# Hybrid encoder layer on one core: identity and filter inputs loaded with their neighbours, and the head of the kernel written in another order

## The chip, the cores and the metric

The kernel runs on one core of a Trainium2 chip. The metric is the device time in microseconds of one execution. "Before" is the kernel as it stood, "after" the changed one.

## What is computed

One encoder layer for two request groups (512 tokens and 256 tokens, 768 in all) with one set of weights, width 1024, then a last norm. Cut to what the head of the kernel needs:

```python
mod = c_act @ w_ada[l] + b_ada[l]
sh1, sc1, g1, sh2, sc2, g2 = jnp.split(mod, 6, axis=-1)
h = modulate(rmsnorm(x, norm1_g[l]), sh1, sc1)      # h * (1 + scale) + shift
proj = h @ w_in[l]                                   # attention, Hyena branch, gates
...
z = jnp.concatenate([t, jnp.cos(fr * w), -jnp.sin(fr * w)], axis=-1)   # positions, 33 wide
h = jnp.sin(f1 * (z @ w1 + b1))                      # implicit filter, layer 0
h = jnp.sin(f2 * (h @ w2 + b2))                      # layer 1
h = (h @ w3)
```

The rest (windowed attention, long convolutions through a transform, merge, squared-ReLU MLP, final norm) comes behind it and is not touched.

## The kernel before, in words

Each of the five engines has one instruction list, written out by hand in the order in which it runs; semaphores join them. Activations lie transposed: 128 features by 768 tokens to a slice, `KD` = 8 slices (`k` = 0 to 7). An output tile `t` is the product of one weight tile (512 KB, 8 slices of 128x128) with all slices. Full precision is had by splitting each operand in a high and a low part: for each slice, three products (`w_hi` with the high activations, `w_hi` with the low ones, `w_lo` with the high ones) in two column pieces, six matmuls into `acc_ps` (line 750). Two tiles (slots 0 and 1 of `acc_ps`) are made side by side in the head, by `first(s, k)` for slot `s` and slice `k` (L901 and behind); the third tile has buffers of its own (`w_third_hilo`), and with it begins the plain run of tile after tile.

The head, up to the third tile, has these parts:

- *Loads.* SyncE's queue: the small vectors `vecT`, the even slices of x, then modulation pieces and the first weight tiles. GpSimd's queue: the odd slices of x and the other modulation pieces. ScalarE's queue: the 128x128 identity (`ident`, L1270), the filter's two first weights (L1271), the positions (`filt_zh`, 33 rows, L1272) and the attention sink. The modulation weights for shift and scale of the first norm come in 16 pieces of 512 KB: group `g` (0 to 3) has pieces 4g to 4g+3 and serves slices 2g and 2g+1. Eleven pieces have room at once; the later ones reuse the places of the first.
- *Norm.* ScalarE squares the eight slices of x (`square`, L1298); VectorE sums them (`norm_acc`, `n_acc`, L1751 and L1754); TensorE sums over the features (`norm_sum`, L816); ScalarE takes the root, VectorE the reciprocal (L1770), TensorE spreads it over the partitions (`norm_spread`, L824). VectorE multiplies each slice (`norm_t`, `xT_in`, L1783), ScalarE scales and shifts it (`norm_h`, `n_h`, L1322) and rounds it (`norm_hi`, `act_hilo`, L1328), VectorE makes the low part (`norm_lo`, L1787).
- *Modulation.* For each group TensorE multiplies eight pieces' halves (`mod_row`, L789), ScalarE copies the rows (`mod_rows`, L1361), TensorE turns them (`mod_turn`, L797), VectorE adds biases (`mod_out`, L1817 to L1820). `norm_h` of slices 2g and 2g+1 waits for group g.
- *Filter.* Layer 0: products of positions and weights (`filt_mlp(0)`, L846), then on VectorE the argument of the sine reduced to one turn in seven steps over 768 columns (`arg_first` L1857, `arg_turns` L1865 and L1866, `arg_rest` L1874, `arg_clamp` L1879 and L1880), the sine on ScalarE (L1372). Layer 1 the same (`filt_mlp(1)`, L848).
- *Unread products.* `warm(n)` (L803) multiplies the identity by ones, 256 columns, and nobody reads the result. Ten of them stand between the sums of squares. In the trace each is two records.

ScalarE loads a function table (`ACT_TABLE_LOAD`) where it changes between sigmoid, root and sine; three times in the head.

## Time and profile before

| | us |
|---|---|
| median of 3 timed runs | 1111.06 (1111.06 to 1111.72) |
| the profiled execution's own time | 1114.14 |
| its span in the profile | 1112.6 |
| TensorE busy | 1092.2 |
| VectorE busy | 802.3 |
| ScalarE busy | 454.5 |

The span runs from the first to the last instruction; the execution's own time has about 1.5 us around it. Matmul records are modelled at their ends and overlap, so a busy TensorE is not one at its peak; a line of the timeline merges neighbouring records of one kind.

### The profile page before, as it was taken

To read this page: it belongs to the slowest core of one execution; us is meant where nothing else is said; L and a number is where in the kernel's file an instruction comes from. 1 tells how busy PE (TensorE), PEld (TensorE's weight loads), DVE (VectorE), ACT (ScalarE), POOL (GpSimd) and SP (SyncE) were. 2 spreads that over 40 slices of the span, in tenths; PEclk is the share of its full clock that TensorE was granted. 3 is DMA by queue.
4 is the path that set the end of the run, shared out by engine and by line. 5 is a ranking of instruction groups with operands and counts; after the bars stand their busy time and mean duration, and the time that the engine had idled before them with its cause. 6 is when DMAs were issued, how large, how long until landed. Compare 5 with 4: busy or idle time off the path is not lost.

```text
span 1112.6 us, 16634 instructions
## 1 busy us (share of the span) xinstructions
PE 1092.2 (98%) x6304; PEld 1022.2 (92%) x6304; DVE 802.3 (72%) x1334; ACT 454.5 (41%) x792; POOL 108.9 (10%) x132
## 2 busy tenths in 40 slices
PE   6999999999999999999999999999999999999997
PEld 4787798888899999999899999999999999999886
DVE  5777699889388685556455777787978778788534
ACT  5631156665722322423246232253442526157414
POOL 2101200000334322000000000000000000000000
PEclk9999999999999999999999999999999999999998
DMA  9923454333332333753312331143333232222303
GB/s 345 394 86 117 154 189 143 129 127 114 119 123 105 119 104 124 282 153 108 110 57 95 125 121 57 57 152 99 111 103 106 95 109 91 87 76 76 95 19 115
DMA packets 45525, 138.85 MB, mean 125 GB/s; under 512 B 5051, under 2 KB 10635, under 8 KB 44556
## 3 DMA queue, kind: packets, MB, share of 16 engines
q1 hardware_dynamic: 29024, 80.21, 21.6%
q0 software_dynamic: 11376, 44.84, 11.3%
q10 hardware_dynamic: 5052, 12.81, 3.3%
q8 instruction: 47, 0.77, 0.3%
q14 instruction: 26, 0.21, 0.1%
HBM read 121.61 MB, written 15.74 MB: 123 GB/s over the span
## 4 chain that ended last, share of the span: by engine, by line
PE 93%; DVE 4%; DMA 1%; ACT 1%; issue 0%; ACTq 0%; DVEq 0%
PE acc_ps L750 39%; PE wk L1181 16%; PE acc_ps L1200 12%; PE acc_ps L832 12%; PE wk L1056 2%; PE acc_ps L839 1%; PE wk L991 1%; PE wk L980 1%; PE wk L970 1%; PE wk L1022 1%; PE wk L872 1%; PE wk L885 1%; DVE dot_out L1832 1%; DMA filt_zh<-in_t_z 1%; PE wk L803 1%; PE wk L890 1%
## 5 line engine op out<-in xcount | busy, mean ns | idle before, releaser
L750 PE MATMUL acc_ps<-act_hilo,w_hi 128*128 128x384 f32 x1504 | 332.5, 342 | 0.1
L750 PEld LDWEIGHTS acc_ps<-act_hilo,w_hi 128*128 128x128 f32 x1504 | 264.8, 189 | 18.8 <-issue 17.7
L750 PE MATMUL acc_ps<-act_hilo,w_lo 128*128 128x384 f32 x752 | 191.5, 335 | 0.0
L750 PEld LDWEIGHTS acc_ps<-act_hilo,w_lo 128*128 128x128 f32 x752 | 136.4, 188 | 0.0
L1200 PE MATMUL acc_ps<-hidden_hilo,act_hilo 128*128 128x384 f32 x768 | 134.6, 335 | 0.2
L1200 PEld LDWEIGHTS acc_ps<-hidden_hilo,act_hilo 128*128 128x128 f32 x768 | 133.2, 188 | 1.1 <-issue 1.1
L1741 DVE TENSOR_TENSOR w_lo<-w_raw,w_hi 128x1024 fp32r<-128x1024 f32 x61 | 76.3, 1252 | 55.1 <-ACT w_hi L1282 54.1
L1282 ACT ACTIVATE w_hi<-w_raw 128x1024 fp32r<-128x1024 f32 x61 | 64.2, 1053 | 44.3 <-PE acc_ps L750 40.9
L2198 DVE SCALAR_TENSOR_TENSOR xT<-acc_ps,modT,xT 128x512 f32<-128x512 f32 (+1 forms) x32 | 19.7, 617 | 59.7 <-PE acc_ps L832 59.5
L1832 DVE CUSTOM_DVE_ANT_0 dot_out<-dot_ring,c_rows,vecT 128x1024 f32<-128x1024 f32 x48 | 61.6, 1284 | 1.6 <-issue 0.6
L2323 DVE SCALAR_TENSOR_TENSOR xT<-acc_ps,modT,xT 128x384 f32<-128x384 f32 (+2 forms) x96 | 40.5, 478 | 28.8 <-PE acc_ps L1200 28.8
L750 PE MATMUL acc_ps<-hidden_hilo,w_hi 128*128 128x384 f32 x256 | 54.7, 334 | 0.0
L1515 ACT ACTIVATE gates_out<-acc_ps 128x768 f32<-128x768 f32 x16 | 13.0, 813 | 98.3 <-PE acc_ps L750 98.3
L832 PE MATMUL acc_ps<-hidden_hilo,w_down_hilo 128*128 128x512 f32 (+1 forms) x288 | 50.2, 336 | 0.0
L832 PEld LDWEIGHTS acc_ps<-hidden_hilo,w_down_hilo 128*128 128x128 f32 x288 | 44.4, 190 | 5.6
L1181 PE MATMUL wk<-act_hilo,w_hi 128*128 128x384 f32 x192 | 48.7, 334 | 0.0
L1181 PE MATMUL wk<-t_hilo,w_hi 128*128 128x384 f32 x192 | 48.7, 334 | 0.0
L2305 DVE TENSOR_TENSOR c_st<-wk,c_st 128x384 f32<-128x384 f32 x84 | 44.9, 551 | 2.7 <-PE wk L1181 2.3
L750 PEld LDWEIGHTS acc_ps<-hidden_hilo,w_hi 128*128 128x128 f32 x256 | 45.3, 188 | 0.0
L1614 ACT ACTIVATE act_hilo<-w_raw 128x512 fp32r<-128x512 f32 x32 | 20.0, 626 | 59.0 <-PE acc_ps L1200 59.0
L2312 DVE TENSOR_TENSOR hidden_hilo<-c_st,hidden_hilo 128x384 fp32r<-128x384 f32 x48 | 26.8, 558 | 22.5 <-ACT hidden_hilo L1633 22.2
L1605 ACT ACTIVATE w_hi<-s_sum 128x512 fp32r<-128x512 f32 x24 | 14.9, 628 | 64.1 <-DVE s_sum L2280 64.1
(301 smaller groups left out, 2026.4 us busy)
## 6 DMA issues: line engine op xcount, KB each, us to landing
w_raw<-in_w_pre SPq DMA_DIRECT2D x50, 512.0 KB, 3.5
dot_ring<-in_w_ada_cols POOLq DMA_DIRECT2D x48, 512.0 KB, 3.8
w_raw<-in_w_up SPq DMA_DIRECT2D x32, 512.0 KB, 3.7
w_raw<-in_w_down SPq DMA_DIRECT2D x16, 512.0 KB, 3.4
w_raw<-in_w_down_half SPq DMA_DIRECT2D x32, 256.0 KB, 2.7
spec<-filt_out POOLq DMA_DIRECT2D x12, 512.0 KB, 2.9
gate_spill<-gates_out ACTq DMA_DIRECT2D x16, 384.0 KB, 2.3
hy_spec<-spec SPq DMA_DIRECT2D x12, 512.0 KB, 5.6
```

Source lines behind the costliest of these rows:

```text
L750: mm = pe.matmul(acc_ps[:, slot, 512 * h:512 * h + HALF], w[:, k, :], src[:, x, k, HALF * h:HALF * h + HALF], start=(first and i == 0), st ...
L832: mm = pe.matmul(acc_ps[:, slot, half(h)], w_i[:, k, :], src[:, x, k, half(h)], start=(n == 0 and i == 0), stop=(n == KD - 1 and i == 2))
L1056: mm = pe.matmul(wk[:, c + o:c + o + P], w, x, start=(i == 0), stop=(i == 1))
L1181: mm = pe.matmul(st_ps(q, j), w[:, k, :], st_act(j, x, k), start=(k == 0 and i == 0), stop=(k == PK - 1 and i == 2))
L1200: mm = pe.matmul(acc_ps[:, m % 2, 512 * h:512 * h + HALF], w[:, k, :], hid[:, x, k, HALF * h:HALF * h + HALF], start=(k == 0 and i == 0), ...
L1282: act_e.activation(whi[s][:] if to is None else to[0], raw[s][:], ACT.Copy).then_inc(hi_done, 1)
L1614: act_e.activation(st_weight(ST_DOWN[m % 3])[0], quarter(m % 4), ACT.Copy).then_inc(sd_hi, 1)
L1741: dve.tensor_tensor(lo, raw[s][:], hi, ALU.subtract).then_inc(lo_done, 1)
L1832: dve.tensor_tensor_reduce(junk[:], ring[:, i], cb[:, g], 1.0, vT[:, V_BA + mt:V_BA + mt + 1], ALU.mult, ALU.add, modT[:, mt, g:g + 1]).th ...
L2305: dve.tensor_tensor(dst, st_ps(q, j), other, ALU.add).then_inc(st_u, 1)
L2312: dve.tensor_tensor(hid_block(q, b, 1), c_block(b), hid_block(q, b, 0), ALU.subtract).then_inc(h4_lo, 1)
L2323: last = dve.scalar_tensor_tensor(xT[:, m, a:b], acc_piece(s, a, b), modT[:, G2 + m, g:g + 1], xT[:, m, a:b], ALU.mult, ALU.add)
```

## The change

1. The identity becomes 128 further columns of the vectors' file (`vecT`), and is no load of its own. The positions and the filter's two weights become one file of 64 rows of 960 numbers (`filt_in`), one load, first in ScalarE's queue. The positions are computed as before, in a function `positions`.
2. SyncE's list: modulation piece 3 moves to it from GpSimd's list, the first weight tile stands behind pieces 1 and 3, the second behind 5 and 7.
3. TensorE: layer 0's products first; layer 1's between the sums of squares in place of unread products (six of the ten stay ahead of the norm); two rows of group 0 ahead of the norm's sum; four unread products, into `acc_ps`, between the halves of group 1's rows; the second weight tile's first products each one place earlier.
4. VectorE: layer 0's argument steps among the first two sums of squares, layer 1's first three steps around the reciprocal.
5. ScalarE: the sine's table first, then the root's behind the squares, then the sine's again behind `act_hilo` of slice 5; layer 0's sine between the squares; rows of group 0 copied ahead of the first weight tile's split, the second tile's split behind the rows of group 1.

```diff
@@ sync
             sp.dma_start(vT[:], a["vec"]).then_inc(ld_vec, 16)
             for k in range(0, KD, 2):
                 x_load(sp, k)
-            mod_load(sp, 1)
+            for p in (1, 3):
+                mod_load(sp, p)
             weights(0)
+            for p in (5, 7):
+                mod_load(sp, p)
             weights(1)
-            for p in range(5, 4 * MODS, 2):
+            for p in range(9, 4 * MODS, 2):
                 mod_load(sp, p)
@@ gpsimd
-            for p in (0, 2, 3, *range(4, 4 * MODS, 2)):
+            for p in range(0, 4 * MODS, 2):
                 mod_load(pool, p)
@@ tensor
-            pe.wait_ge(ld_ident, 16)
+            pe.wait_ge(ld_filt, 16)
+            filt_mlp(0)
+            pe.wait_ge(ld_vec, 16)
             turn_c()
-            pe.wait_ge(ld_filt, 32)
-            filt_mlp(0)
             pe.wait_ge(ones_set, 2)
-            for k in range(2, KD - 1):
+            for k in range(2, 6):
                 pe.wait_ge(n_acc, k)
-                warm(2)
+                if k == 3:
+                    pe.wait_ge(f_sin, 1)
+                    filt_mlp(1)
+                else:
+                    warm(2)
+            for k in range(2):
+                mod_row(0, k)
             norm_sum(0)
-            for k in range(KD):
+            for k in range(2, KD):
                 mod_row(0, k)
             norm_spread(0)
             mod_turn(0)
             for k in range(4):
                 mod_row(1, k)
-            pe.wait_ge(f_sin, 1)
-            filt_mlp(1)
+            warm(4, acc_ps[:, 0, 0:256])
             for k in range(4, KD):
                 mod_row(1, k)
             first(0, 0)
             mod_turn(1)
             first(0, 1)
+            first(1, 0)
             for k in range(KD):
                 mod_row(2, k)
-            first(1, 0)
+            first(1, 1)
             mod_turn(2)
             first(0, 2)
-            first(1, 1)
@@ scalar
-            act_e.dma_start(ident[:], a["t_ident"]).then_inc(ld_ident, 16)
-            act_e.dma_start(fw12[:], a["filt_w12"]).then_inc(ld_filt, 16)
-            act_e.dma_start(zh[0:33, :], a["t_z"]).then_inc(ld_filt, 16)
+            act_e.dma_start(fin[:], a["filt_in"]).then_inc(ld_filt, 16)
...
-            act_e.activation(rs[:, 0:1], epsc[:], ACT.Sqrt).then_inc(sqrt_set, 1)
+            act_e.activation(es[:, 0, 0:1], epsc[:], ACT.Sin)
+            square(0)
+            square(1)
             act_e.wait_ge(c_turned, 1)
...
-            for k in range(KD):
+            square(2)
+            square(3)
+            act_e.wait_ge(f_arg, 1)
+            act_e.activation(h1[:], fb[0:64, :], ACT.Sin).then_inc(f_sin, 1)
+            for k in range(4, KD):
                 square(k)
+            act_e.activation(rs[:, 0:1], epsc[:], ACT.Sqrt).then_inc(sqrt_set, 1)
             act_e.wait_ge(sqrt_set, 1)
             norm_std(0)
-            act_e.activation(es[:, 0, 0:1], epsc[:], ACT.Sin)
+            mod_rows(0)
             split_w(0)
-            mod_rows(0)
-            split_w(1)
-            act_e.wait_ge(f_arg, 1)
-            act_e.activation(h1[:], fb[0:64, :], ACT.Sin).then_inc(f_sin, 1)
             norm_h(0)
             norm_hi(0)
             norm_h(1)
             norm_hi(1)
             mod_rows(1)
+            split_w(1)
...
             norm_hi(5)
+            act_e.activation(es[:, 0, 0:1], epsc[:], ACT.Sin)
@@ vector
-            for k in range(KD):
-                norm_acc(k)
             arg_first(0)
             arg_turns(0)
+            norm_acc(0)
+            arg_rest(0)
+            norm_acc(1)
+            arg_clamp(0)
+            for k in range(2, KD):
+                norm_acc(k)
+            arg_first(1)
             norm_rstd(0)
-            arg_rest(0)
-            arg_clamp(0)
+            arg_turns(1)
             norm_t(0)
...
             mod_out(1)
-            arg_first(1)
             split_w(1)
...
             norm_t(5)
-            arg_turns(1)
             norm_lo(4)
```

On TensorE, the head of its list up to the spread of the norm. Before (line, operation, out<-in, shape and count; `ident` is the identity, `mod_raw` and `c_padded` make the rows of the modulation):

```order
L809 MATMUL wk<-ident,c_act 16x128
L846 MATMUL acc_ps<-filt_zh,filt_w 64x512
L846 MATMUL acc_ps<-filt_zh,filt_w 64x256
L803 MATMUL wk<-ones,ident 128x256 x10
L816 MATMUL wk<-ones,n_acc 128x1 x6
L789 MATMUL wk<-mod_raw,c_padded 32x512 x8
L824 MATMUL wk<-ident,norm_rstd 128x128 x6
```

and after:

```order
L849 MATMUL acc_ps<-filt_in 64x512
L849 MATMUL acc_ps<-filt_in 64x256
L812 MATMUL wk<-vecT,c_act 16x128
L806 MATMUL wk<-ones,vecT 128x256 x2
L851 MATMUL acc_ps<-filt_h,filt_in 128x512
L851 MATMUL acc_ps<-filt_h,filt_in 128x256
L806 MATMUL wk<-ones,vecT 128x256 x4
L792 MATMUL wk<-mod_raw,c_padded 32x512 x2
L819 MATMUL wk<-ones,n_acc 128x1 x6
L792 MATMUL wk<-mod_raw,c_padded 32x512 x6
L827 MATMUL wk<-vecT,norm_rstd 128x128 x6
```

Layer 1's products and two rows of group 0 now stand ahead of the norm's sum, four of the unread products no longer do.

On VectorE, the same place, from the first sum of squares to the first normalised slice. Before:

```order
L1751 COPY n_acc<-n_sq 128x768
L1754 TENSOR_TENSOR n_acc<-n_acc,n_sq 128x768 x7
L1857 TENSOR_SCALAR filt_arg<-acc_ps,vecT 64x768
L1865 TENSOR_SCALAR filt_turn<-filt_arg 64x768
L1866 TENSOR_SCALAR filt_turn<-filt_turn 64x768
L1770 RECIPROCAL norm_rstd<-norm_rstd 128x6
L1874 SCALAR_TENSOR_TENSOR filt_red<-filt_turn,filt_arg 64x768
L1874 SCALAR_TENSOR_TENSOR filt_red<-filt_turn,filt_red 64x768
L1879 SCALAR_TENSOR_TENSOR filt_red<-filt_turn,filt_red 64x768
L1880 TENSOR_SCALAR filt_red<-filt_red 64x768
L1783 TENSOR_TENSOR xT_in<-xT_in,wk 128x768
```

and after, to the reciprocal:

```order
L1868 TENSOR_SCALAR filt_arg<-acc_ps,vecT 64x768
L1876 TENSOR_SCALAR filt_turn<-filt_arg 64x768
L1877 TENSOR_SCALAR filt_turn<-filt_turn 64x768
L1762 COPY n_acc<-n_sq 128x768
L1885 SCALAR_TENSOR_TENSOR filt_red<-filt_turn,filt_arg 64x768
L1885 SCALAR_TENSOR_TENSOR filt_red<-filt_turn,filt_red 64x768
L1765 TENSOR_TENSOR n_acc<-n_acc,n_sq 128x768
L1890 SCALAR_TENSOR_TENSOR filt_red<-filt_turn,filt_red 64x768
L1891 TENSOR_SCALAR filt_red<-filt_red 64x768
L1765 TENSOR_TENSOR n_acc<-n_acc,n_sq 128x768 x6
L1868 TENSOR_SCALAR filt_arg<-acc_ps,vecT 128x768
L1781 RECIPROCAL norm_rstd<-norm_rstd 128x6
```

All seven steps of layer 0 now stand ahead of the last six sums, and the first step of layer 1 ahead of the reciprocal.

On ScalarE, the last slices of the norm. After:

```order
L1328 ACTIVATE n_h<-xT_in,modT,norm_scale 128x512
L1328 ACTIVATE n_h<-xT_in,modT,norm_scale 128x256
L1363 ACTIVATE mod_rows<-wk 128x512
L1334 ACTIVATE act_hilo<-n_h 128x768
L1398 ACT_TABLE_LOAD
L1398 ACTIVATE att_sinke<-eps 128x1
L1328 ACTIVATE n_h<-xT_in,modT,norm_scale 128x512
L1328 ACTIVATE n_h<-xT_in,modT,norm_scale 128x256
```

The first two rows are slice 5, the last two slice 6; the table load and the one-column sine between them are new here, the rest stood so before.

## Rows read from the trace of the kernel before

**Rows 1.** The page: the span, and TensorE's busy time

```profile
span 1112.6 us, 16634 instructions
...
PE 1092.2 (98%) x6304; PEld 1022.2 (92%) x6304; DVE 802.3 (72%) x1334; ACT 454.5 (41%) x792; POOL 108.9 (10%) x132
```

**Rows 2.** Busy time by stretches (us): PE, PEld, DVE, ACT, POOL, clock, DMA share, GB/s

```profile
20.00:25.00 5.00, 5.00 (x43) 3.44 (x43) 4.39 (x8) 4.00 (x6) 1.05 (x2) 1.00 1.03 409
...
56.00:1106.00 1050.00, 1046.48 (x6062) 988.91 (x6060) 760.00 (x1266) 415.47 (x736) 96.30 (x103) 1.00 0.33 111
```

**Rows 3.** The chain that ended last, 0 to 70 us: start, us, what

```profile
1.91 7.76 DMA filt_zh<-in_t_z
...
9.71 2.82 PE acc_ps L846 x4
12.53 7.12 PE wk L803 x20
...
46.08 21.13 PE acc_ps L750 x120
```

**Rows 4.** Line 803, the unread products: duration ns min/median/max, first and last start

```profile
L803 PE MATMUL wk<-ones,ident x20: 379/634/795, 12.5 to 19.3; 128*128 128x256 f32 x20
```

**Rows 5.** Busy time by stretches, columns as in rows 2, around the clock's fall

```profile
34.90:38.20 3.30, 2.17 (x18) 1.81 (x14) 2.44 (x4) 2.52 (x4) 0.00 (x0) 1.00 1.02 402
38.30:41.60 3.30, 3.30 (x12) 3.30 (x12) 3.00 (x7) 2.16 (x4) 2.58 (x5) 0.50 0.79 265
```

**Rows 6.** Timeline of VectorE: start us, us, what, idle before and its releaser

```profile
16.70 2.02 DVE L1754 TENSOR_TENSOR n_acc<-n_acc,n_sq 128x768 f32<-128x768 f32 x2 [0.30 <-ACT n_sq L1298]
...
18.64 1.06 DVE L1857 TENSOR_SCALAR filt_arg<-acc_ps,vecT 64x768 f32<-64x768 f32 x1
...
21.35 0.19 DVE L1770 RECIPROCAL norm_rstd<-norm_rstd 128x6 f32<-128x6 f32 x1 [0.48 <-ACT norm_rstd L1313]
...
24.84 0.94 DVE L1783 TENSOR_TENSOR xT_in<-xT_in,wk 128x768 f32<-128x768 f32 x1
```

**Rows 7.** Timeline of ScalarE, columns as in rows 6

```profile
15.82 1.58 ACT L1298 ACTIVATE n_sq<-xT_in 128x768 f32<-128x768 f32 x2 [0.74 <-DMA xT_in<-in_x_T]
...
21.26 1.28 ACT L1367 ACT_TABLE_LOAD   x1
22.55 0.20 ACT L1367 ACTIVATE att_sinke<-eps 128x1 f32<-128x1 f32 x1
...
27.48 0.84 ACT L1328 ACTIVATE act_hilo<-n_h 128x768 fp32r<-128x768 f32 x1
...
47.20 1.31 ACT L1322 ACTIVATE n_h<-xT_in,modT,norm_scale 128x512 f32<-128x512 f32 x2 [1.68 <-issue]
```

**Rows 8.** Timeline of TensorE, columns as in rows 6

```profile
19.48 1.40 PE L816 MATMUL wk<-ones,n_acc 128*128 128x1 f32 x12
...
28.55 1.14 PE L789 MATMUL wk<-mod_raw_b,c_padded 128*32 128x512 f32 x8
...
30.94 1.05 PE L797 MATMUL wk<-vecT,mod_rows 128*128 128x2 f32 x8
...
37.38 1.11 PE L797 MATMUL wk<-vecT,mod_rows 128*128 128x2 f32 x8 [1.14 <-ACT mod_rows L1361]
...
42.12 1.48 PE L789 MATMUL wk<-mod_raw,c_padded 128*32 128x512 f32 x10
...
45.13 0.95 PE L797 MATMUL wk<-vecT,mod_rows 128*128 128x2 f32 x8
...
56.53 8.59 PE L750 MATMUL acc_ps<-act_hilo,w_third_hilo 128*128 128x384 f32 x48
```

**Rows 9.** DMA issues up to 60 us (KB, us to landing), and GpSimd's wait

```profile
ident<-in_t_ident ACTq DMA_DIRECT2D x1, 64.0 KB, 2.4
...
sink<-in_attn_sink ACTq DMA_DIRECT2D x1, 4.0 KB, 10.1
...
38.27 0.53 POOL L621 DMA_DIRECT2D filt_w<-in_filt_w  x1 [14.60 <-DMA mod_raw_c<-in_w_ada_rows]
```

More of the change, by code:

```diff
@@ L2529, in _, with positions @@
                     y_half(k - 1)
+def positions():
+    import numpy as np
+    f = np.float32
+    zs = []
+    for L in (TS, TP):
+        t = np.linspace(0.0, 1.0, L, dtype=f)
+        w = (f(2.0 * PI) * np.arange(L, dtype=f) / f(L)).astype(f)
+        fr = np.linspace(1e-4, 15, 16, dtype=f)
+        fw = (fr[:, None] * w[None, :]).astype(f).astype(np.float64)
+        zs.append(np.concatenate([t[None].astype(np.float64), np.cos(fw), -np.sin(fw)], axis=0))
+    return np.concatenate(zs, axis=1).astype(f)
 def tables():
```

53 lines of the change are left out of this document (24 added, 29 removed).

## The prediction, made before the changed kernel ran

> **What bounds the kernel now.** I read the page first: TensorE is busy 1092.2 of 1112.6 us [rows 1]. The busy time by stretches says where the rest lies: from 56 to 1106 us it is busy 1046.5 of 1050 us [rows 2]. So whatever the change does, it does in the head, and it is worth as much as it moves one event: the first product of the third weight tile, at 56.53 us [rows 8]. From there on TensorE works through an unchanged list.
>
> The chain of waits through the head begins with a transfer: the positions of the filter land 7.76 us after their issue at 1.91 us, then four products take 2.8 us, then twenty records of the unread products 7.1 us [rows 3]. These last are at half speed to begin with: one takes 634 ns in the middle case and 379 ns in the fastest [rows 4]. The profile's clock column prints 1.00 there, but the durations show 1.2 GHz until about 17.7 us, after TensorE had worked since 9.7 us; then it is at 2.4 GHz. It falls once more: 0.50 from 38.3 to 41.6 us, after the stretch 34.9 to 38.2 in which TensorE was busy only 2.17 of 3.3 us [rows 5]; it sat idle 1.14 us for the copied rows of modulation group 2 [rows 8]. The fall costs about half of 3.4 us, 1.7 us.
>
> From 46.1 us on the chain is TensorE alone [rows 3]. Before that, it goes through VectorE and ScalarE: sum of squares ready at 18.7 us, first normalised slice begun at 24.84 us [rows 6], and each slice then through `n_h` and `act_hilo` on ScalarE [rows 7]. The last modulation piece has landed by 38.3 us, when GpSimd stops waiting for it [rows 9]; group 3's rows start only at 42.12 us [rows 8], so the transfers do not bound the end of the head.
>
> **The change, part by part.**
>
> *Loads.* Three transfers of 211 KB on ScalarE's queue become one of 64 rows of 3,840 bytes (240 KB), the vectors grow from 81 to 145 KB: 93 KB more, 0.23 us at the 409 GB/s of 20 to 25 us [rows 2]. When the filter's file lands, no row shows. Lower bound: like the unit matrix, also first in that queue, 2.4 us after its issue at 0.9 us [rows 9], so 3.3 us. Upper: like the positions, 7.8 us after issue, so 8.7 us. It is first in its queue and has only 4 rows for each of 16 engines, so it is nearer the first: I take 3.9 us.
>
> *Filter, layer 0.* Four products of 2.8 us end at 6.7 us. VectorE's seven argument steps took from 18.64 to 24.84 us less the reciprocal of 0.19 us and the 0.48 us of waiting ahead of it, 5.5 us [rows 6], behind the sums of squares. Now they stand ahead of sums 3 to 8. 6.7 + 5.5 + two sums (0.6 and 1.0) and the waits between them end at 13.9; six sums every 1.06 us (two take 2.02 [rows 6]) end at 20.2 us. Before it was 18.7 us: the transfer of x, whose last pair of squares starts at 15.82 [rows 7], no longer bounds this, VectorE does: **+1.5 us**.
>
> *TensorE before the norm.* Six unread products instead of ten stand ahead of the sum, but layer 1's products now too, and two rows of group 0. Sine ready at about 14.7; layer 1 has as many records and columns as layer 0, which took 2.8 us with its tail at 1.2 GHz [rows 3], so 2.6 us to the next product, to 17.3; four unread products are eight records, 3.4 us at 1.2 GHz or 1.7 us at full clock (634 - 379 is the 0.2 us by which one is longer [rows 4]). If the clock rises at about 19.5 us, they end at 20.2, two rows take 0.9: the sum starts at 21.1 us instead of 19.48 [rows 8], **+1.6 us**. (A rise at 17.7 gives 20.3, none before 21.2 gives 22.2.)
>
> *From the norm to group 3.* The spread moves by the same 1.6. But VectorE had held the first `xT_in` until 24.84 [rows 6] with arguments that are now done, so that one moves only to 25.8 (+1.0), and the turn of group 1 goes from 30.94 [rows 8] to 32.0 (+1.1). Landings: a piece of 512 KB takes 1.28 us at 409 GB/s, 2.56 us while two queues share. The last of x landed at 15.8 [rows 7], 16.05 now; SyncE's list behind it (pieces 1, 3, weight 0, 5, 7, weight 1, 9) gives weight 1 at 31.4, needed at 33, and piece 9 at 34.0; then GpSimd's queue is done, and 11 follows at 35.5, 15 at 38.1. Rows of group 2 run 35.7 to 37.5, behind slice 0 of the second tile, which followed them before. Then the second tile's slice 1 (1.04 us) fills the 1.14 us of idleness, and the clock need not fall: group 3's rows start at 40.5, not 42.12, **-1.6 us**.
>
> *The unread four* (1.7 us, from 27.5 us) end at 29.2 while TensorE would wait for the last piece of group 1, which before came at about 28.6 [rows 8] and now 0.24 later, and for VectorE. They cost nothing; without that cover they would cost at most 1.7.
>
> *What is late next.* Rows of group 3 end at 42.3, but ScalarE copies them only behind `n_h` of slice 5. That one follows the scale of group 2 (ready on VectorE at 40.2) by two `n_h` (1.3 us each) and one `act_hilo` (0.8) [rows 7]: copy 43.6 to 44.2. So the turn moves from 45.13 only to 44.3: **-0.8 us**. From there 10.4 us of products in either kernel lead to the third tile: its start 56.53 becomes 55.7 us. VectorE finishes the last slices one ahead of TensorE, by about 0.7 us as now.
>
> *Table loads.* Four instead of three, 1.28 us each and 0.2 for what follows [rows 7]. The sine's stands ahead of the first square, as the root's did; the root's lies after the last square, while TensorE works; the new one, 1.5 us, lies behind `act_hilo` 5, where ScalarE was idle for 1.68 us [rows 7]: nothing. In the rows the next operation starts 1.29 us after the load began. The Trainium skill (ScalarE: Activation LUTs, What ACT_TABLE_LOAD costs) adds a drain of some 1.4 us to each switch; the trace does not bear it out. By it slices 6 and 7 would be 1.2 us later with 0.7 us of slack, so the sum 0.5 us worse.
>
> **The sum.** -0.8 us against the profiled execution's own 1114.14 us. The timed runs lie 3.1 us below that one, at 1111.06 us. Whether they had the fall of 1.7 us is not recorded. If they had, the forecast is 1110.3; if not, their third tile began at 54.8 and the change makes it 55.7: 1112.0. In the middle **1111.2 us**. No change, that is: about 0.2% (2.2 us) is what a measurement tells from none.
>
> **Rivals.**
>
> *Slower: the clock rises late.* Now TensorE worked without a break from 9.71 until 17.7 us before it rose. After the change it has layer 0's products until 6.7, nothing until about 12.3, two unread products, a gap, and layer 1's with 64 of 128 rows. If it stays at 1.2 GHz until 24.6 us, the sum starts at 22.2, its 12 records take 2.3 instead of 1.4 us, the six rows 3.4 instead of 1.7, and the third tile starts at about 58.1: +1.6 against the profiled execution, up to +3.3 against runs without the fall, 1114.2 us. It decides from a rise later than about 23 us. For it: the durations of [rows 4]. Against: from 14.7 us TensorE has no gap. The Trainium skill (TensorE: Matmul & The Clock Gate, HAM oscillation) says that gaps between bursts send the clock back to half; the fall at 38.3 us agrees. Chance 0.15.
>
> *Late file.* It lands like the positions did, at 7 us or later. Everything of VectorE's moves with it: sums of squares at 23.1, third tile at 57.7 to 58.2, in time 1112.5 to 1114.0, so 1113.3. For it: even the 4 KB of the sink took 10.1 us [rows 9]; against: those were last in the queue. Chance 0.10.
>
> *Faster.* File at 3.5, clock full by 17.7, third tile at 54.8, and the copy of group 3 not behind `n_h` 5, another 1.1 us: -2.8 us against runs that have the fall, 1108.3 us. For it: 1.7 us of cold clock and 1.14 us of waiting are there to be had [rows 5, 8]. Against: the copy's place in ScalarE's order. Chance 0.12 (0.13 with a little less).
>
> *It does not keep the clock up.* The unread four lie at 27 to 29 us, the fall at 38 us; only the second tile's moved product fills that place. Should the clock fall anyway, 1.7 us come back: 1112.9 us. This lies inside the forecast's 0.62.
>
> **Chances.** Forecast 0.62, all within 0.2%. Late clock 0.15: 0.12 slower, 0.03 same. Late file 0.10: 0.06 and 0.04. Faster 0.13: 0.12 and 0.01. So faster 0.12, same 0.70, slower 0.18. The range takes in the late clock and the edge of the faster case: 1108.9 to 1114.5 us.
>
> **What would show it.** The filter's file landed by 4 us (layer 0's products start there); last sum of squares at about 20; TensorE's sum of them at 21; records of the unread products at 634 or 379 ns; no 0.50 in the clock column at 38 us; group 3's rows at 40.5; the third tile at 55.7. A third tile before 54.3 or after 57.9, or a different idle time behind 56 us, would make the prediction wrong.

## The result, and the profile after

The changed kernel takes **1117.88 us** (median of 6, 1117.33 to 1120.74); the kernel before took 1111.39 us beside it (1111.01 to 1113.94). The ratio is 1.0056, 95% interval 1.0041 to 1.0071: some 6 us slower, where no change was forecast. The profiled execution took 1117.58 us. Its page, span and busy time, as in [rows 1]:

```profile
span 1115.9 us, 16636 instructions
...
PE 1092.6 (98%) x6304; PEld 1020.1 (91%) x6304; DVE 802.0 (72%) x1334; ACT 456.4 (41%) x794; POOL 108.4 (10%) x131
```

The engines do the same work. The busy time by stretches of the changed kernel, columns as in [rows 2]:

```profile
9.00:14.00 5.00, 0.00 (x0) 0.00 (x0) 4.83 (x8) 1.60 (x3) 0.00 (x0) 1.00 1.03 411
...
59.00:1109.00 1050.00, 1046.02 (x6058) 988.51 (x6058) 759.31 (x1265) 415.00 (x735) 96.30 (x103) 1.00 0.34 111
...
38.30:41.60 3.30, 3.30 (x25) 1.61 (x24) 1.82 (x2) 2.24 (x5) 2.16 (x5) 1.00 0.98 330
```

Behind 59 us TensorE is as busy as before, and there is no fall of the clock at 38 us. TensorE does nothing at all from 9 to 14 us, while VectorE is busy for 4.83 of these 5 us. What it does shows on its timeline (columns as in rows 6):

```profile
8.38 1.07 DVE L1868 TENSOR_SCALAR filt_arg<-acc_ps,vecT 64x768 f32<-64x768 f32 x1 [3.72 <-PE acc_ps L849]
...
10.66 0.56 DVE L1762 COPY n_acc<-n_sq 128x768 f32<-128x768 f32 x1
...
13.10 0.96 DVE L1765 TENSOR_TENSOR n_acc<-n_acc,n_sq 128x768 f32<-128x768 f32 x1
...
14.95 0.55 DVE L1891 TENSOR_SCALAR filt_red<-filt_red 64x768 f32<-64x768 f32 x1
15.43 6.26 DVE L1765 TENSOR_TENSOR n_acc<-n_acc,n_sq 128x768 f32<-128x768 f32 x6
...
25.66 0.19 DVE L1781 RECIPROCAL norm_rstd<-norm_rstd 128x6 f32<-128x6 f32 x1 [2.99 <-ACT norm_rstd L1319]
...
28.68 0.95 DVE L1794 TENSOR_TENSOR xT_in<-xT_in,wk 128x768 f32<-128x768 f32 x1 [1.80 <-PE wk L827]
```

The last six sums run back to back and end at 21.7 us: VectorE is the engine that is late, no longer the transfer of x. Behind them it has spare time, 2.99 and 1.80 us, where before it made the first `xT_in` late. ScalarE waits for it with the squares, which have two buffers:

```profile
11.32 0.84 ACT L1304 ACTIVATE n_sq<-xT_in 128x768 f32<-128x768 f32 x1 [1.56 <-DVE n_acc L1762]
14.15 0.84 ACT L1304 ACTIVATE n_sq<-xT_in 128x768 f32<-128x768 f32 x1 [1.99 <-DVE n_acc L1765]
15.54 0.84 ACT L1374 ACTIVATE filt_h<-filt_red 64x768 f32<-64x768 f32 x1 [0.54 <-DVE filt_red L1891]
...
48.06 1.28 ACT L1398 ACT_TABLE_LOAD   x1
49.35 0.20 ACT L1398 ACTIVATE att_sinke<-eps 128x1 f32<-128x1 f32 x1
49.73 1.31 ACT L1328 ACTIVATE n_h<-xT_in,modT,norm_scale 128x512 f32<-128x512 f32 x2 [0.17 <-issue]
```

And TensorE's timeline, the places of [rows 8]:

```profile
5.53 2.82 PE L849 MATMUL acc_ps<-filt_in 33*64 33x512 f32 x4 [5.53 <-DMA filt_in<-in_filt_in]
...
14.20 2.05 PE L806 MATMUL wk<-ones,vecT 128*128 128x256 f32 x4 [5.32 <-DVE n_acc L1765]
16.52 2.90 PE L851 MATMUL acc_ps<-filt_h,filt_in 64*128 64x512 f32 x4 [0.27 <-ACT filt_h L1374]
19.35 3.43 PE L806 MATMUL wk<-ones,vecT 128*128 128x256 f32 x8
22.71 1.05 PE L792 MATMUL wk<-mod_raw,c_padded 128*32 128x512 f32 x4
23.70 1.50 PE L819 MATMUL wk<-ones,n_acc 128*128 128x1 f32 x12
...
30.28 1.99 PE L806 MATMUL acc_ps<-ones,vecT 128*128 128x256 f32 x8
...
37.49 0.93 PE L753 MATMUL acc_ps<-act_hilo,w_hi 128*128 128x384 f32 x4 [0.48 <-issue]
...
47.36 1.05 PE L800 MATMUL wk<-vecT,mod_rows 128*128 128x2 f32 x8 [0.46 <-ACT mod_rows L1363]
...
59.04 2.18 PE L753 MATMUL acc_ps<-act_hilo,w_third_hilo 128*128 128x384 f32 x11
```

From 16.52 to 23.70 us it has no gap, but runs at 1.2 GHz almost to the end: the eight records from 19.35 us take 3.43 us. The trace's record of the clock has its first stretch at full speed from 22.3 us on; the clock column of the views prints 1.00 ahead of that too, as in the kernel before. The norm's sum starts 2.0 us behind the end of the last sum of squares, and 1.0 us of this are the two rows of group 0 (22.71 to 23.70). The filter's file is first in its queue, and in the DMA issues (KB, us to landing) stands

```profile
filt_in<-in_filt_in ACTq DMA_DIRECT2D x1, 240.0 KB, 4.6
```

so it landed at 5.49 us.

### The profile page after: what moved, and what is told of

It is laid out like the page before. It is cut to its first block, busy times and chain, and to the rows that moved or that the text cites. A ratio compares the mean times of both kernels' runs of the same rounds, so it can differ in the third digit from the quotient of the medians.

```text
span 1115.9 us, 16636 instructions
## 1 busy us (share of the span) xinstructions
PE 1092.6 (98%) x6304; PEld 1020.1 (91%) x6304; DVE 802.0 (72%) x1334; ACT 456.4 (41%) x794; POOL 108.4 (10%) x131
## 3 DMA queue, kind: packets, MB, share of 16 engines
q1 hardware_dynamic: 29168, 80.80, 22.3%
## 4 chain that ended last, share of the span: by engine, by line
PE 91%; DVE 3%; ACT 1%; issue 1%; DMA 1%; DVEq 0%; ACTq 0%
PE acc_ps L753 39%; PE wk L1189 16%; PE acc_ps L1208 12%; PE acc_ps L835 12%; PE wk L1064 2%; PE acc_ps L842 1%; PE wk L999 1%; PE wk L988 1%; PE wk L978 1%; PE wk L1030 1%; PE wk L875 1%; PE wk L888 1%; DVE dot_out L1843 1%; PE wk L893 1%; DMA spec<-filt_out 1%
## 5 line engine op out<-in xcount | busy, mean ns | idle before, releaser
L2336 DVE SCALAR_TENSOR_TENSOR xT<-acc_ps,modT,xT 128x384 f32<-128x384 f32 (+2 forms) x96 | 40.5, 478 | 28.8 <-PE acc_ps L1208 28.8
```

What stands on the lines that cost most here:

```text
L2336: last = dve.scalar_tensor_tensor(xT[:, m, a:b], acc_piece(s, a, b), modT[:, G2 + m, g:g + 1], xT[:, m, a:b], ALU.mult, ALU.add)
```

## The experiments

Fourteen runs, e1 to e14. Each time stands against the median of the kernel before on the same chip. The table gives, for the profiled execution of each, where an event starts (us, from the timelines): the last sum of squares on VectorE, the norm's sum and spread and the turns of groups 1 to 3 on TensorE, the third tile. The last column is the start of the first stretch at full speed in the trace's record of the clock.

| kernel | last sum of squares | norm's sum | spread | turn 1 | turn 2 | turn 3 | third tile | clock first rises |
|---|---|---|---|---|---|---|---|---|
| before (1114.14, rows above) | 17.8 | 19.48 | 22.66 | 30.94 | 37.38 | 45.13 | 56.53 | 17.8 |
| e1, before again (1111.64) | 16.8 | 18.51 | 21.69 | 29.97 | 36.41 | 42.59 | 54.05 | 16.0 |
| e6, files only | 17.2 | 18.19 | 21.97 | 30.18 | 36.52 | 42.72 | 54.02 | 16.1 |
| e13, arguments alone | 20.9 | 21.89 | 25.18 | 33.20 | 39.63 | 45.82 | 57.11 | 19.1 |
| after | 20.7 | 23.70 | 26.96 | 34.79 | 41.70 | 47.36 | 59.04 | 22.3 |
| e7, queues back | 20.4 | 24.23 | 27.50 | 35.32 | 42.24 | 47.89 | 59.58 | 23.8 |
| e3, six products more | 20.3 | 21.35 | 25.89 | 34.09 | 42.58 | 48.23 | 59.91 | 13.0 |
| e8, three steps less | 17.7 | 21.83 | 25.10 | 32.93 | 39.84 | 45.49 | 57.17 | 21.0 |
| e9, both of these | 17.5 | 18.56 | 21.83 | 31.03 | 38.12 | 43.77 | 55.46 | 11.5 |
| e10, sum first | 20.0 | 20.98 | 26.78 | 34.60 | 41.53 | 47.18 | 58.88 | 26.3 |
| e5, filter back | 17.4 | 19.22 | 22.49 | 30.78 | 38.79 | 44.45 | 55.85 | 16.1 |
| e11, second tile back too | 17.9 | 19.25 | 22.52 | 30.91 | 37.25 | 43.42 | 54.72 | 15.8 |
| e12, group 2 ahead | 17.2 | 18.19 | 22.54 | 30.32 | 36.10 | 42.18 | 53.47 | 16.1 |
| e14, copies ahead | 17.6 | 18.58 | 22.81 | 30.59 | 35.73 | 41.81 | 53.68 | 16.9 |

### What the profiled execution of before stands for: e1

The kernel before, unchanged, once more.

> The kernel before, unchanged, to see how much of the gap between the two kernels the profiled execution of before hides. In its first trace the clock fell to half from 38.3 to 41.6 us and the third weight tile began at 56.53 us, and that execution took 1114.14 us where the others took 1111.0 to 1111.7. If the fall belongs to the slower executions, as I think, a trace of this kernel without a fall has the third tile at about 54 to 55 us and a time of 1111.1. If the rival holds (the fall is in all of them and the 3 us are the profiler's), the fall shows again, with 1111.1 beside it.

1112.01 against 1112.93 us, ratio 0.9998 (0.9988 to 1.0007). Its profiled execution took 1111.64 us, 2.5 us less than that of [rows 1], and its busy time by stretches around the place of [rows 5] is

```profile
34.10:37.40 3.30, 2.17 (x15) 1.85 (x15) 2.44 (x4) 2.52 (x4) 0.00 (x0) 1.00 1.03 405
37.40:40.70 3.30, 3.30 (x25) 2.35 (x28) 2.85 (x7) 2.23 (x4) 2.68 (x5) 1.00 0.69 217
```

while its timeline of TensorE has

```profile
18.51 1.40 PE L816 MATMUL wk<-ones,n_acc 128*128 128x1 f32 x12
...
36.41 1.05 PE L797 MATMUL wk<-vecT,mod_rows 128*128 128x2 f32 x8 [1.13 <-ACT mod_rows L1361]
...
54.05 2.15 PE L750 MATMUL acc_ps<-act_hilo,w_third_hilo 128*128 128x384 f32 x11
```

The same idle time of 1.13 us and the same 2.17 us of work in 3.3 us, and no fall of the clock. So the fall belongs to a part of the executions of before. This trace, like that of the changed kernel, has no fall in the head, and is the one to compare with: the third tile is 5.0 us later after the change, and 5.2 us of delay are already there at the norm's sum.

### Parts of the change on the kernel before: e2, e6, e13

**e2**: files and queue order of the change, every engine's order as before.

```diff
-            mod_load(sp, 1)
+            for p in (1, 3):
+                mod_load(sp, p)
             weights(0)
+            for p in (5, 7):
+                mod_load(sp, p)
             weights(1)
...
-            for p in (0, 2, 3, *range(4, 4 * MODS, 2)):
+            for p in range(0, 4 * MODS, 2):
```

> The kernel before with the loads of the change alone: the identity in the vectors' file, one file for the filter (lying in another free place), the new order of pieces on the two queues; all engines' lists as before. If the reordered head costs the 6.5 us, this is 1110.5 to 1112 us, with the filter's file at about 5.5 us and the sum of squares at about 19 us. If the loads cost it (piece 9, piece 11 and the second weight land later, x later), it is 1114 or more, with idle time ahead of group 2's rows.

1121.7 against 1112.93 us, ratio 1.008 (1.0065 to 1.0095). ScalarE's timeline:

```profile
31.21 1.06 ACT L1283 ACTIVATE w_hi<-w_raw 128x1024 fp32r<-128x1024 f32 x1 [6.13 <-DMA w_raw<-in_w_pre]
```

The second weight tile now lands behind four pieces, and before's order has its split ahead of slice 0's scaling: 6.13 us of waiting, the clock falls from 26.2 to 39.9 us, third tile at 63.71. That price belongs to the mixture, not to the change, which moves that split.

**e6**: the files only.

```diff
-            act_e.dma_start(ident[:], a["t_ident"]).then_inc(ld_ident, 16)
-            act_e.dma_start(fw12[:], a["filt_w12"]).then_inc(ld_filt, 16)
-            act_e.dma_start(zh[0:33, :], a["t_z"]).then_inc(ld_filt, 16)
+            act_e.dma_start(fin[:], a["filt_in"]).then_inc(ld_filt, 16)
```

> The kernel before with the merged files alone (identity in the vectors' file, one filter file first in ScalarE's queue), queues of pieces and all engines' lists as before. If the 9 to 10 us of the second run were the blocked split of the second weight, this is 1110.5 to 1112.5 us, and the first n_h starts near 25.5 us. If larger files cost by themselves (x or the vectors landing 1 us late), 1113 or more.

1113.03 against 1112.96 us, ratio 0.9999 (0.999 to 1.0009), third tile at 54.02. The merged files are worth nothing by themselves; the file landed at 5.92 us, and from here on e6 serves as the base.

**e13**: e6, and on VectorE alone layer 0's arguments ahead.

```diff
-            for k in range(KD):
-                norm_acc(k)
             arg_first(0)
             arg_turns(0)
-            norm_rstd(0)
+            norm_acc(0)
             arg_rest(0)
+            norm_acc(1)
             arg_clamp(0)
+            for k in range(2, KD):
+                norm_acc(k)
+            norm_rstd(0)
```

> One part of the change alone, on the version with merged files (run e6, which is as fast as before): only VectorE's order, layer 0's seven argument steps ahead of and among the first two sums of squares. Every other engine stays as before (TensorE: the two loads' products, ten unread products, sum; layer 1's products behind the norm; ScalarE: squares, root, split, sine). Theory (VectorE's 5.5 us of arguments push the sums of squares, and the norm's sum with them, and nothing behind gives it back): last sum starts at 20.5 to 21.5 us instead of 17.2, the norm's sum at 22 to 22.5 instead of 18.2 if the clock has risen, third tile 2 to 4 us later (the first normalised slice no longer waits 1 us for arguments, so 3), at 56.5 to 58, time 1115 to 1116.5 against some 1112.5. Rival (the modulation pieces and the split's order bound the head, the norm has slack): third tile at 54 to 55, time as e6.

1115.26 against 1111.85 us, ratio 1.0027 (1.0016 to 1.0037). Timelines of VectorE and TensorE:

```profile
15.58 6.26 DVE L1752 TENSOR_TENSOR n_acc<-n_acc,n_sq 128x768 f32<-128x768 f32 x6
...
14.35 2.04 PE L803 MATMUL wk<-ones,vecT 128*128 128x256 f32 x4 [5.85 <-DVE n_acc L1752]
16.57 4.97 PE L803 MATMUL wk<-ones,vecT 128*128 128x256 f32 x16 [0.18 <-DVE n_acc L1752]
21.89 1.50 PE L816 MATMUL wk<-ones,n_acc 128*128 128x1 f32 x12 [0.35 <-DVE n_acc L1752]
```

VectorE's order alone moves the last sum of squares by 3.7 us and the third tile by 3.1 (57.11 against 54.02); by the ratio, too, it is 3 us slower. The norm has no slack. Its TensorE was idle for 5.85 us too, yet with ten unread products and nothing else ahead of the sum it follows the last sum of squares at once.

### Parts taken off the changed kernel: e3, e8, e9, e10, e7

**e3**: six unread products into the gap.

```diff
             pe.wait_ge(ones_set, 2)
+            warm(6)
```

> The changed kernel with six more unread products right behind layer 0's, where TensorE is idle from 8.9 to 14.2 us. If the late rise of the clock (22.3 us instead of 17.8) costs a good part, the clock rises by 18 to 19 us, the norm's sum starts at 22.6 or earlier instead of 23.7, and 1.5 to 2.5 us come back: 1115.5 to 1116.5. If VectorE's order costs nearly all, the sum of squares still ends at 21.7 us and under 1 us comes back: 1117 or more.

1116.04 against 1112.93 us, ratio 1.003 (1.002 to 1.0041); 11 runs, from 1114.63 to 1119.40. The clock is up at 13.0 us and the norm's sum starts at 21.35, right behind VectorE: 2.35 us earlier than after (0.4 of this because its filter file landed earlier). But the profiled execution, the longest of them, lost the clock twice; by stretches:

```profile
19.50:22.90 3.40, 2.62 (x21) 1.68 (x24) 2.68 (x3) 2.09 (x3) 0.00 (x0) 1.00 1.03 410
23.30:26.70 3.40, 3.40 (x16) 1.08 (x9) 1.19 (x3) 0.68 (x2) 0.94 (x2) 0.50 1.02 407
```

**e8**: three of layer 0's seven steps left out (the filter's values differ).

```diff
             def arg_rest(layer):
+                if layer == 0:
+                    return
...
-                chain(dve.scalar_tensor_tensor(fb[h], fk[h], -TWO_PI_C, fb[h], ALU.mult, ALU.add))
+                if layer:
+                    chain(dve.scalar_tensor_tensor(fb[h], fk[h], -TWO_PI_C, fb[h], ALU.mult, ALU.add))
```

> The changed kernel without three of layer 0's seven argument steps (the two that take off whole turns and the first half of the last; the filter's values are then others). If VectorE's list bounds the sums of squares, they end about 2.9 us earlier, at 18.8 us. If that alone carries on, the third tile starts near 56 us: 1114.5 to 1115.5. If TensorE at half speed is the second bound behind it (six unread products, layer 1 and two rows ahead of the norm's sum), the sum starts only 1.5 to 2 us earlier, and it is 1115.5 to 1116.5.

1115.74 against 1112.96 us, ratio 1.0026 (1.0016 to 1.0035). TensorE:

```profile
17.04 3.78 PE L806 MATMUL wk<-ones,vecT 128*128 128x256 f32 x8
...
21.83 1.50 PE L819 MATMUL wk<-ones,n_acc 128*128 128x1 f32 x12
```

The sums are 3.0 us earlier, the norm's sum and the third tile only 1.9: TensorE, at half speed, ends later than VectorE. So there are two bounds close to each other.

**e9**: e3's and e8's edits together (the same three steps left out).

```diff
             pe.wait_ge(ones_set, 2)
+            warm(6)
...
+                if layer == 0:
+                    return
```

> The kernel after, with both of the edits that each gave back a part: three of layer 0's seven argument steps left out on VectorE (the two of L1885 and the first of L1890; the filter's values differ, so this leaves out part of the computation), and six unread products behind the turn of c, so that TensorE is not idle ahead of the sums. Theory (two bounds on the norm's sum, VectorE's 5.5 us of arguments and TensorE at half speed behind its idleness): the sums end at 18.8 us and TensorE, at full clock, starts the norm's sum within 0.7 us of that, at 19.5; third tile at about 55, time 1113 to 1113.8 against 1115.74 and 1116.04 with one edit each. Rival (one bound only, the other edit's gain is the same gain): 1115.5 to 1116. If the clock falls again in the gap behind the six products: 1115.

1114.63 against 1112.09 us, ratio 1.0024 (1.0014 to 1.0033). The norm's sum starts at 18.56 us, as before, 5.1 us earlier than after: each bound had hidden the other. The third tile gains only 3.6 of it, and the time lay 0.8 us above what I expected. TensorE and ScalarE:

```profile
25.86 1.05 PE L792 MATMUL wk<-mod_raw_b,c_padded 128*32 128x512 f32 x4 [0.66 <-DMA mod_raw_b<-in_w_ada_rows]
...
31.41 1.06 ACT L1289 ACTIVATE w_hi<-w_raw 128x1024 fp32r<-128x1024 f32 x1 [0.81 <-DMA w_raw<-in_w_pre]
```

With the norm as early as before, group 1's piece and the second weight tile land late: the transfers are a third bound. I read this from the two waits; no run takes it away. The rival's size (1115.5 or more) did not come either. By the ratios alone (1.0024 and 1.0026) e9 cannot be told from e8; the norm's sum tells them apart.

**e10**: nothing but layer 1's products between the sine and the norm's sum.

```diff
-            for k in range(2, 6):
+            for k in range(2, 4):
...
-            for k in range(2):
-                mod_row(0, k)
             norm_sum(0)
-            for k in range(2, KD):
+            for k in range(KD):
                 mod_row(0, k)
```

> The kernel after without the unread products behind the fourth and fifth sum and with all rows of group 0 behind the norm's sum, as before: nothing but layer 1's products is between the sine and the norm's sum. Theory (VectorE's late sums are the first bound, at 21.7 us; TensorE's queue adds 1.3 to 2 us): the norm's sum starts at 21.9, but at half speed, since TensorE was idle before it: its twelve records take 2.3 instead of 1.4 us and the rows 3.4 instead of 1.8; third tile 58 to 59, time 1116.5 to 1117.9. Rival (the unread products and the rows are what costs, the rest of the order is harmless): third tile at 57.2, time 1116 or less.

1119.25 against 1112.09 us, ratio 1.0061 (1.0046 to 1.0077).

```profile
17.61 1.06 PE L851 MATMUL acc_ps<-filt_h,filt_in 64*128 64x256 f32 x2
20.98 2.72 PE L819 MATMUL wk<-ones,n_acc 128*128 128x1 f32 x12 [2.32 <-DVE n_acc L1763]
23.63 3.22 PE L792 MATMUL wk<-mod_raw,c_padded 128*32 128x512 f32 x16
26.78 1.60 PE L827 MATMUL wk<-vecT,norm_rstd 128*128 128x128 f32 x12
```

The norm's sum is 2.7 us earlier (0.8 of it because the filter's file landed earlier), the spread behind it only 0.2: sum and rows at 1.2 GHz take 2.72 and 3.22 us, where e13 took 1.50 and 1.92 for them. The clock rises at 26.3 us. From the end of the last sum of squares to the spread it takes 5.9 us, after took 5.3. So the unread products and the two rows cost 2 us in the queue, and leaving them out costs at least as much in the clock. The third tile (58.88) is where the theory had it; the time lies 1.4 us above its range, and by the ratios (1.0061 and 1.0056) e10 cannot be told from after.

**e7**: both queues in the order of before.

```diff
-            for p in (1, 3):
-                mod_load(sp, p)
+            mod_load(sp, 1)
             weights(0)
```

> The changed kernel with the pieces and weights in their old order on SyncE's and GpSimd's queues. If the queue order of the change is harmless to its own lists, as its trace says (rows of group 2 wait for nothing at 38.7 us, long after piece 11 at 33.7), it stays at 1117 to 1118.5 us. If landings bound the changed head, 1116 or less, or above 1119.

1117.49 against 1112.96 us, ratio 1.0042 (1.0027 to 1.0056), third tile at 59.58: the order of the queues is not the cause. This run shows something else as well. Its filter file landed 0.8 us earlier than after's, at 4.7 us, and still its clock rose later, at 23.8 us. TensorE:

```profile
13.87 2.04 PE L803 MATMUL wk<-ones,vecT 128*128 128x256 f32 x4 [5.77 <-DVE n_acc L1762]
19.02 3.78 PE L803 MATMUL wk<-ones,vecT 128*128 128x256 f32 x8
```

The stretch without work is as long as after's (5.77 against 5.32 us), for the arguments and the sums behind it start with the file too.

### The filter back at its place, the other moves kept: e4, e5, e11

**e4**: TensorE, ScalarE and VectorE have the filter's steps where they stood; the two rows ahead of the norm's sum, the second tile's moves and the queues stay.

```diff
-                if k == 3:
-                    pe.wait_ge(f_sin, 1)
-                    filt_mlp(1)
-                else:
-                    warm(2)
+                warm(2)
...
-            warm(4, acc_ps[:, 0, 0:256])
+            pe.wait_ge(f_sin, 1)
+            filt_mlp(1)
```

> The changed kernel with the filter's steps where they were (layer 0's argument behind the sums of squares, its sine behind the split of the weights, layer 1 in group 1's rows, ten unread products, no unread four; ScalarE's and VectorE's lists as before). Loads, layer 0's products first, two rows ahead of the norm's sum and the second tile's products one place earlier stay. If the filter's place on VectorE ahead of the sums is the cause, the sums end at 18.7 to 19 us and it is 1109.5 to 1111.5. If TensorE's moved rows and products are the cause it stays above 1114.

1124.86 against 1112.93 us, ratio 1.0099 (1.0081 to 1.0118), third tile at 66.30. It took ScalarE's list of before whole, and with it e2's blocked split: a mistake of the experiment, so it says nothing on the filter's place. **e5** mends it:

```diff
-            split_w(0)
             mod_rows(0)
-            split_w(1)
+            split_w(0)
...
             mod_rows(1)
+            split_w(1)
```

> The fourth run again (filter's steps back in their old places on VectorE, ScalarE and TensorE, all other moves of the change kept), with one repair: in the fourth run ScalarE's old list asked for the second weight at 25 us, which the new queue order lands at 30 to 31 us; here its split stands behind the rows of group 1, as in the change. If the filter's place ahead of the sums is the cause of the 5 us in the head, the sums end by 18.5 us, the first normalised slice starts at 24 to 25 us, the third tile at 54 to 55.5 us, and it is 1111 to 1113 us. If TensorE's moves or the queue order cost by themselves, the third tile stays at 57 us or later and the time at 1115 or more.

1114.49 against 1112.96 us, ratio 1.0024 (1.001 to 1.0039). The norm's sum is back at 19.22 us and the third tile 3.2 us earlier than after: most of the 5.0 us, but third tile and time lie above both ranges of the theory (55.85 and 1114.49 us). The norm's sum starts 0.8 us behind the end of the last sum of squares (18.39 us), where e6's followed at once: the two rows of group 0, now ahead of it, take 1.0 us. The rest of what remains shows on TensorE:

```profile
34.58 0.93 PE L753 MATMUL acc_ps<-act_hilo,w_hi 128*128 128x384 f32 x4 [1.59 <-DVE w_lo L1744]
...
35.79 1.48 PE L792 MATMUL wk<-mod_raw_b,c_padded 128*32 128x512 f32 x10
```

The second tile's slice 0, now ahead of group 2's rows, waits for the low part of its weights, and the rows wait behind it. **e11** puts it back:

```diff
             first(0, 1)
-            first(1, 0)
             for k in range(KD):
                 mod_row(2, k)
-            first(1, 1)
+            first(1, 0)
             mod_turn(2)
             first(0, 2)
+            first(1, 1)
```

> The kernel with the filter's steps at their old places (run e5, 1114.49 us), and now also the second tile's first two slices at their old places on TensorE: slice 0 behind group 2's rows, slice 1 behind slice 2 of the first tile. Theory (of e5's remaining 1.5 us, most is the second tile's slice 0 ahead of group 2's rows: it waits for the split of the second weight tile, which now stands behind group 1's rows, and the rows stand behind it, 35.8 instead of 32.1 us): group 2's rows at 32 to 33, third tile 54.3 to 54.8, time 1113.0 to 1113.5. Rival (it is the landing of the modulation pieces in the new queue order): group 2's rows stay at 34 or later, time 1114.2 to 1114.8.

1113.22 against 1112.09 us, ratio 1.0009 (0.9999 to 1.0018); group 2's rows start at 32.97 us, third tile at 54.72, 1.1 us earlier than e5. It confirms the place. In the changed kernel itself the same wait is only 0.48 us (at 37.49). There layer 1's argument step is already done, and the weights had the time of the late norm to land; that these are the reasons is argued, not shown.

### A version that beats both? e12, e14

In e1 ScalarE copies the rows of group 2, ready at 34.1 us, only behind slice 3's scaling at 35.78, and TensorE waits 1.13 us for them. **e12** is e6 with this (and slice 3's multiplication ahead of the second tile's split on VectorE):

```diff
-            norm_h(3)
             mod_rows(2)
+            norm_h(3)
...
-            norm_lo(3)
             mod_out(2)
+            norm_lo(3)
```

> A version meant to beat both: the kernel before with the two merged files only (run e6, 1113.03 against 1113.0), and group 2 served sooner. ScalarE copies group 2's rows ahead of slice 3's scaling instead of behind it; VectorE multiplies slice 3 ahead of layer 1's first argument step and the second tile's split, and adds group 2's biases ahead of slice 3's low part. In the trace of the kernel before, undisturbed, the rows of group 2 ended at 34.1, the copy began at 35.8 behind slice 3's scaling, and the turn at 36.4; the biases followed at 38.0 and slice 4 at 38.4. Theory (the head between the spread and the third tile is a chain turn, biases, scaling, not transfers): turn of group 2 at 35, slice 4's scaling at 36.9, third tile 0.8 to 1.5 us earlier, at 52.6 to 53.3, ratio to before 0.9987 to 0.9993. Rival (the pieces of group 3 land at 37 to 38 us and bound the end): turn of group 2 earlier, third tile the same, ratio 1.000.

1111.39 against 1112.09 us, ratio 0.9995 (0.9986 to 1.0004), third tile at 53.47: less than hoped. The turn of group 2 is only 0.4 us earlier than e6's. TensorE now waits 0.60 us for the split instead:

```profile
34.98 0.93 PE L750 MATMUL acc_ps<-act_hilo,w_hi 128*128 128x384 f32 x4 [0.60 <-issue]
```

**e14** leaves slice 3 where it was and serves group 3 in the same way.

```diff
-            norm_h(5)
             mod_rows(3)
+            norm_h(5)
...
-            norm_lo(5)
             mod_out(3)
+            norm_lo(5)
```

> Second try at a version that beats both. Run e12 (1111.39 against 1112.09, ratio 0.9995 with an interval that holds 1) got the turn of group 2 only 0.4 us earlier, since slice 3's multiplication, put ahead of the second tile's split on VectorE, let TensorE wait 0.6 us for that split with slice 0 of the second tile, which stands ahead of the turn. Now VectorE keeps slice 3 where it was; ScalarE copies the rows of group 2 ahead of slice 3's scaling and those of group 3 ahead of slice 5's, and VectorE adds the biases of groups 2 and 3 ahead of slice 3's and slice 5's low part. Theory (the chain turn, biases, scaling bounds the end of the head): turn of group 2 at 35.0, slice 4's scaling at 37, turn of group 3 at 41, third tile at 52.5 to 53.2, 0.8 to 1.5 us ahead of e6's 54.02, ratio 0.9985 to 0.9993. Rival (TensorE waits for the low part of slice 3 instead, since the biases stand ahead of it, or the last piece lands at 37 to 38 us and group 3's rows wait for it): third tile at 53.5 to 54, ratio 0.9995 to 1.

1111.35 against 1111.85 us (11 runs), ratio **0.9992** (0.9983 to 1.0001). ScalarE and TensorE:

```profile
34.80 0.60 ACT L1359 ACTIVATE mod_rows<-wk 128x512 f32<-128x512 f32 x1 [0.49 <-PE wk L789]
35.29 1.30 ACT L1320 ACTIVATE n_h<-xT_in,modT,norm_scale 128x512 f32<-128x512 f32 x2
...
35.73 0.95 PE L797 MATMUL wk<-vecT,mod_rows 128*128 128x2 f32 x8
```

From the spread to the third tile it takes 30.9 us, e6 took 32.0; 0.8 of this was lost ahead of the spread in the profiled execution, half at the norm's sum and half in group 0's rows, which took 2.87 us against 2.42. e12 took 30.9 us as well, so serving group 3 sooner gained nothing more, and the third tile (53.68) lies where the rival had it. It beats the changed kernel by 6 us. That it beats the one before is not shown: the interval just holds 1.

## Why the prediction was wrong

The place was right: everything happens ahead of the third tile, and the chain goes through the norm's sum. The steps:

1. *"I take 3.9 us" for the landing of the filter's file.* It was 5.49 us, 4.6 us after its issue; in the runs with the same file 3.7 to 5.0 us. I had bounds of 2.4 and 7.8 us from [rows 3, 9] and went to the nearer one by its place in the queue, not by its size, which is nearly four times that of the unit matrix. The Trainium skill (DMA: Bandwidth & Descriptors, Anatomy of one DMA) has a fit for transfers that GpSimd issues: some 2.0 us, and the bytes at 436 GB/s. An estimate by it for 240 KB is 2.6 us; this transfer, issued by ScalarE, took 3.7 to 5.0 us while the other queues loaded x.
2. *The sums "end at 20.2 us", "+1.5 us".* They ended at 21.7. The duration of the seven steps (5.5 us) and the six sums behind each other were right; the 1.5 us between are step 1. But the delay was reckoned from 18.7 us, in an execution whose x landed late; in e1 the sums end at 17.8 us, and the delay is 3.9 us, not 1.5. Measured alone (e13), the order of VectorE costs 3.7 us at the last sum and **3.1 us at the third tile**.
3. *"If the clock rises at about 19.5 us … the sum starts at 21.1".* It rose at 22.3 us and the sum started at 23.7. The sine was ready at 16.4 instead of 14.7 us (step 1 again), and from there on layer 1's products (2.9 us), eight records (3.4) and two rows stood in the queue, nearly all at 1.2 GHz. The text gives the sum at 22.2 us for no rise before; with the sine 1.7 us later that is 23.9, and so it came: the size of the case was right, the choice wrong. Beside e13, where VectorE's sums end at nearly the same time (21.8 us, here 21.7), the changed kernel loses another **1.9 us** at the third tile (59.04 against 57.11). This is a difference of two kernels that differ in the queues, in ScalarE's list and behind the norm too; but 1.8 of it is there at the norm's sum, which in e13 follows the last sum of squares at once, and e3 and e9, with TensorE kept busy, have nearly none of it there. So I put it to TensorE's new order. These two are the 5.0 us.
4. *The rivals.* Late clock (0.15) and late file (0.10) were priced one by one, at 1114.2 and 1113.3 us. Neither came as it was set: the file landed 1.6 us late, not 3, and the clock rose at 22.3 us, where the rival wanted a rise behind 23. Half of each came, and the halves add up: what delays the file delays the sine, and with it the queue of TensorE that runs at 1.2 GHz. The late clock is not the file's doing, though: e7's landed 0.8 us earlier and its clock rose 1.5 us later. The two prices were too low as well. Their third tiles, 58.1 and 57.7 to 58.2, mean 1115.7 and 1115.3 to 1115.8 us by step 6. By the text's own reckoning, too, 3.3 us above 1111.06 are 1114.4 us, not 1114.2.
5. *"Group 3's rows start at 40.5, not 42.12", "-1.6 us".* The 42.12 came from an execution with the fall; without it they start at 39.59 (e1). From the norm's sum to the third tile I had 34.6 us; after the change it is 35.3, in e1 35.5. So all that the change does behind the norm's sum gave 0.2 us. The second tile's moves fill the 1.13 us of waiting for the copy of group 2's rows, and group 3's rows start 20.0 us behind the norm's sum instead of e1's 21.1 (forecast 19.4). But at the turn of group 3 0.4 us of this is left (23.7 against 24.1): its rows' copy stands behind slice 5's scaling, as the text had it, and TensorE waits 0.46 us for it.
6. *"If not, their third tile began at 54.8", and the middle of two cases.* e1 took 1111.64 us with the third tile at 54.05, 1057.6 us from there; the profiled execution of [rows 8] has the same 1057.6 us. So a third tile at 55.7 meant 1113.3 us, not 1111.2. This is the step that counted on a gain: 1.5 of the 2.4 us that the text takes off between the norm's sum and the third tile (37.05 to 34.6) are the fall, which by their mean clock more than half of the executions of before did not have. The fall itself is 1.5 of the 2.5 us between the two, about the 1.7 in the text; 1.0 us was there already at the norm's sum (19.48 against 18.51), since x landed later.
7. *The unread four and the table load*, both costed at nothing: the four end at 32.2 us and group 1's rows behind them at 33.2, when slice 0's low part is ready too, without which TensorE's next product (33.32) can't start. The sine's table is followed 1.29 us later by the next operation (48.06, 49.35), without a drain, while TensorE works through slices 4 and 5. No run took them out of the changed kernel by themselves, so for both this is argued from the trace.

The miss of 6.4 us (1117.58 against 1111.2): 2.6 at the norm's sum (steps 1 to 3, against the forecast's 21.1), 0.7 from there to the third tile (5), 2.1 the baseline (6), and 0.9 behind the third tile, where I had nothing.

What the change costs, against e1: 3.1 + 1.9 = 5.0 us at the third tile; from the third tile's first product to the last one into `acc_ps` 1046.9 against 1046.4 us, 0.5 more, which no run explains; 0.3 us behind it; 0.1 outside the span; 5.9 us between the two profiled executions (1117.58 - 1111.64). The medians of the timed runs are 6.5 us apart.

## What to carry to other kernels

Work that is taken out of a gap on one engine's path must not be put ahead of the reduction that everything waits for: VectorE's arguments held the first normalised slice back by about 0.5 us (e1: spread done at 23.3 us, slice begun at 23.9), and 5.5 us of them ahead of the sums of squares are 3.1 us at the end, however early the sine comes. Before you reckon against a profiled execution, see whether the timed runs look like it; here a clock fall (1.5 us) and a late x (1.0) made it 2.5 us longer, and an edit seemed to win 1.6 us that, by their mean clock, more than half of the runs never lost. And reckon two delays that meet in one engine's queue together, not one by one.

## What the hardware showed that I had not expected

- *The fall of the clock is not a function of the idle time alone.* The kernel before shows 2.17 us of work in 3.3 us at the same place in two executions; one fell to 0.50 behind it, the other stayed at 1.00. The trace with the fall has a mean clock of 0.996, the other 0.998. Of 20 executions of before beside e1 to e4 (a single one took 1350.45 us and is left out) ten have 0.997 or 0.998 and took 1110.76 to 1112.50 us, ten have 0.995 or 0.996 and took 1112.93 to 1115.40 us; beside all fourteen runs it is 54 and 37. The Trainium skill (TensorE: Matmul & The Clock Gate, HAM oscillation) says that gaps send the clock back; e2, e3 and e4 agree, the kernel before does in a part of its executions.
- *More unread products don't settle it.* With six more (e3) the clock rose at 13.0 us, and fell at 23.3 and 36.9 us in the longest execution, 4.8 us above the shortest.
- *A first load of 240 KB takes 3.7 to 5.0 us* from its issue to its landing, at the head of ScalarE's queue.
- *e10's time lies further above its span than the others':* 1119.25 us in the median with spans of 1116.3 to 1117.3 us, 1.7 to 3.3 us outside it, where the changed kernel has 1.6 to 1.7. So about half of its 1.4 us over the changed kernel lies outside the profile, and stays open.
